# Experts: the last block's rows added from the chip, all other rows fetched under its computation, gates applied at the copy

## The reference, cut to what matters

```
# hier_moe(xf [T, 1024], ...):  T = 768 tokens in layer 0 (512 latent + 256 context), 512 in layer 1
# 4 groups x 8 experts; each token picks one group and its 2 best experts
gate = jax.nn.softmax(top_v, axis=-1) * g_val            # one gate per token and choice
# the 2*T (token, choice) pairs are sorted by expert into blocks of rows
yb  = (silu(xblk @ w1[e]) * (xblk @ w3[e])) @ w2[e]      # per block; w1, w3 [1024, 512], w2 [512, 1024]
out = zeros.at[row_tok].add(yb * row_gate[:, None])
# then   x = x + g2 * out        (g2: a scale per channel)
```

## Time and profile before

| | us |
|---|---|
| median of 3 runs (lowest, highest) | 3034.67 (3034.35, 3039.01) |
| the profiled execution | 3035.01 |
| its span in the profile | 3033.1 |
| PE busy in the span | 2746.8 (91%) |
| DVE, ACT, POOL busy | 1291.5, 842.7, 214.4 |
| layer 0: first to last `silu` of the blocks | 1619.98 to 2100.63 |
| layer 1: the same | 2537.55 to 2994.92 |
| least distance of two `silu`s (a block that nothing holds up) | 13.5 |
| the last two distances in layer 0; in layer 1 | 14.61, 15.28; 14.99, 15.75 |

### The profile page before, as it was taken

How to read it: one execution, slowest core, us unless ns; L and a number is a source line. 1 busy time by engine, 2 the same in 40 slices (tenths; PEclk the granted TensorE clock), 3 DMA queues, 4 the chain that set the end, 5 groups by cost and what they waited for, 6 DMA issues and landing times. The chain is left out here.

```text
span 3033.1 us, 33241 instructions
## 1 busy us (share of the span) xinstructions
PE 2746.8 (91%) x12578; PEld 1791.7 (59%) x12578; DVE 1291.5 (43%) x2005; ACT 842.7 (28%) x1404; POOL 214.4 (7%) x304
## 2 busy tenths in 40 slices
PE   7999989999989999899978988987797987998986
PEld 5888867766767888688654433333664553433332
DVE  5776575655456766621452111111647732111112
ACT  3323235454343323322221111111325721111110
POOL 0111100000001111012100000000000000000000
PEclk9999999999999999999988999998898997999998
DMA  5666622211225566511058999998110047999997
GB/s 205 216 223 223 220 77 70 84 58 68 97 76 208 194 213 234 185 55 69 15 210 348 423 426 424 426 427 352 68 48 15 1 203 315 423 426 425 424 426 270
DMA packets 104597, 672.57 MB, mean 222 GB/s; under 512 B 14712, under 2 KB 19192, under 8 KB 50224
## 3 DMA queue, kind: packets, MB, share of 16 engines
q1 hardware_dynamic: 65360, 542.64, 44.4%
q0 software_dynamic: 32800, 105.12, 9.7%
q10 hardware_dynamic: 6336, 23.50, 2.1%
HBM read 685.91 MB, written 24.64 MB: 234 GB/s over the span
## 5 line engine op out<-in xcount | busy, mean ns | idle before, releaser
L2306 DVE TENSOR_TENSOR big<-big,bank 64x512 f32<-64x512 f32 x65 | 44.9, 691 | 811.5 <-ACT big L1543 811.5
L1973 DVE SCALAR_TENSOR_TENSOR tabs<-tabs,tmp 128x1024 f32<-128x1024 f32 x160 | 193.6, 1223 | 174.8 <-DMA tabs<-in_wm 174.4
L949 PE MATMUL bank<-big 128*64 128x512 f32 x464 | 215.9, 620 | 37.1 <-DMA big<-in_w 35.5
L952 PE MATMUL bank<-big 128*64 128x512 f32 x512 | 237.5, 618 | 0.0
L949 PE MATMUL bank<-slot,big 128*64 128x512 f32 x480 | 211.4, 593 | 2.9 <-DMA ar_f<-in_w 2.9
L952 PE MATMUL bank<-ar_f,big 128*64 128x512 f32 x480 | 211.4, 593 | 0.0
L1396 ACT ACTIVATE w_high<-slot 128x1024 fp32r<-128x1024 f32 (+1 forms) x138 | 140.8, 1041 | 203.9 <-DMA slot<-in_w 102.1
L639 PE MATMUL bank<-u_split,w_low 128*128 128x512 f32 x720 | 178.0, 389 | 0.0
L949 PEld LDWEIGHTS bank<-big 128*64 128x64 f32 x464 | 64.5, 143 | 183.2 <-issue 129.0
L965 PE MATMUL bank<-big 128*64 128x512 f32 x560 | 153.9, 701 | 19.2 <-DVE big L2310 19.2
L2736 POOL DMA_DIRECT2D tabs<-in_wm x160 | 84.7, 529 | 1164.8 <-DVE tabs L1973 723.7
(11 more groups left out here) (415 smaller groups left out, 5534.7 us busy)
## 6 DMA issues: line engine op xcount, KB each, us to landing
big<-in_w SPq DMA_DIRECT2D x93, 2048.0 KB
slot<-in_w SPq DMA_DIRECT2D x164, 1024.0 KB, 4.8
tabs<-in_wm POOLq DMA_DIRECT2D x160, 512.0 KB, 4.6
ar_f<-in_w SPq DMA_DIRECT2D x64, 1024.0 KB
tabs<-in_w SPq DMA_DIRECT2D x32, 1024.0 KB
tmp<-in_w SPq DMA_DIRECT2D x32, 1024.0 KB
slot<-in_wd SPq DMA_DIRECT2D x16, 1408.0 KB, 6.4
ar_u<-in_w SPq DMA_DIRECT2D x18, 1024.0 KB, 18.1
```

Source lines behind the costliest of these rows:

```text
L949: ga = nc.tensor.matmul(bank[0][lo, :], xT[:, 4 * c + k, :], w[c][:, k * EF:(k + 1) * EF], **flags)
L952: mm = nc.tensor.matmul(bank[0][hi, :], xT[:, 4 * c + k, :], w[2 + c][:, k * EF:(k + 1) * EF], **flags)
L1973: nc.vector.scalar_tensor_tensor(mslot[m % 2], mslot[m % 2], 1.0, crow, ALU.mult, ALU.mult, accum_out=modf[:, idx:idx + 1]).then_inc(mod_d ...
L2306: nc.vector.tensor_tensor(hmul[MB:2 * MB, :], hsil[MB:2 * MB, :], bank[0][MB:2 * MB, :], ALU.mult).then_inc(q["h_ready"], 1)
```

## The change

1. **Gates.** POOL builds `gate_block`, as `in_block` but with the gate as value, which DVE until now applied to `yrows`. PE multiplies it with `at_place` into a table of gates for each block and row, ACT copies it to `slot_gates`, and `copy_y` applies it as the scale of its copy.
2. **Last block.** It always uses the third set. The registers are set so that the last loop has one block less and the pairs may be one less. SP issues its six loads with no wait. The last loop's wait number is now `2 * n - 1`, which for the first of its blocks means the block before the block before.
3. **Selection.** DVE builds `last_sel`, 64 x 768, one where a row of the last block belongs to a token. At the end PE computes a tile's sum transposed as a product of the fetched rows with the identity plus a product of `ysb`'s rows with `last_sel`. The last block is not scattered.
4. **Fetch.** SP waits for `y_last`, now the scatter of the last block but one, and issues all fetches while the last block is computed. In layer 0 it issues two loads for the attention among them. The meeting of the engines there is gone.
5. **Zeros.** Rows of `yb` that belong to the last block are not written, so POOL clears both layers' `yb` (2 x 6.3 MB) from a tile of zeros after the layer `even_in`.

```diff
@@ SP, stream_experts
+                def fetch(t):
+                    for x in range(2):
+                        rows_of = d["yb"][l][x * SC + t * P:x * SC + t * P + P, :]
+                        sp.dma_start(yrows[t][x], rows_of).then_inc(got[t], 16)
...
+                sp.wait_ge(q["route_sums"], route_sum(l, "gates"))
                 for c in ORDER[4:]:
                     load(c, e2, 2)
...
-                with sp.Fori(2 * pairs + rotated, last + 1) as b:
-                    block_of(b, b, 1)
-                sp.wait_ge(q["gate_full"], last + 1)
+                with sp.Fori(pairs + rotated // 2, last - pairs - rotated // 2) as n:
+                    block_of(nc.s_assert_within(n + pairs + rotated // 2, 14, NBMAX - 2), 2 * n - 1, 1)
+                e_last = sp.value_load(exp_i[0:1, bass.ds(last, 1)], min_val=0, max_val=NE - 1)
+                for c in ORDER:
+                    load(c, e_last, 2)
+                sp.wait_ge(tload[1], 32 * (rotated // 3 + 1) * (l + 1))
+                sp.wait_ge(q["y_last"], 16 * (l + 1))
+                for t in range(LT):
+                    fetch(t)
+                if l == 0:
+                    for c in range(2):
+                        qkv_load(c)
+                    for t in range(LT, TT):
+                        fetch(t)
@@ PE, moe_layer
+                pe.wait_ge(gates_in, l + 1)
+                for n in range(2 * nt):
+                    mm = nc.tensor.matmul(bank[3][:, 0:TABW], at_place[:, n, :], gate_block[:, n, :], start=(n == 0), stop=(n == 2 * nt - 1))
+                mm.then_inc(q["route_sums"], 1)
...
-                phase.end()
+                block(last, in_third(rotated // 3), None, None)
...
+                    if t == 0:
+                        pe.wait_ge(q["sel_ready"], l + 1)
+                        pe.wait_ge(q["y_ready"], last + 1)
                     for k in range(KT):
-                        tr = nc.tensor.transpose(bank[2 * (t % 2) + k // 4][:, (k % 4) * P:(k % 4 + 1) * P],
-                                                 yrows[t][0][:, k * P:(k + 1) * P], ident)
+                        out_k = bank[2 * (t % 2) + k // 4][:, (k % 4) * P:(k % 4 + 1) * P]
+                        nc.tensor.matmul(out_k, yrows[t][0][:, k * P:(k + 1) * P], ident, start=True, stop=False)
+                        tr = nc.tensor.matmul(out_k, ysb[lo, k * P:(k + 1) * P], last_sel[:, t * P:(t + 1) * P], start=False, stop=True)
@@ ACT, moe_layer
-                    nc.scalar.activation(ysb[rows, 0:EF], bank[4][0:MB, :], ACT.Copy)
-                    nc.scalar.activation(ysb[rows, EF:D], bank[4][MB:2 * MB, :], ACT.Copy).then_inc(q["y_ready"], 1)
+                    for n, half in enumerate((slice(0, MB), slice(MB, 2 * MB))):
+                        i = nc.scalar.activation(ysb[rows, n * EF:(n + 1) * EF], bank[4][half, :], ACT.Identity,
+                                                 scale=slot_gates[half, bass.ds(at, 1)])
+                    i.then_inc(q["y_ready"], 1)
...
+                silu(last)
                 act.wait_ge(q["y_last"], 16 * (l + 1))
-                phase.end()
-                for t in range(nt):
-                    if t > 1:
-                        act.wait_ge(q[f"got{t % 2}"], 32 * ((TT * l + t) // 2))
-                    for x in range(2):
-                        rows_of = d["yb"][l][x * SC + t * P:x * SC + t * P + P, :]
-                        act.dma_start(yrows[t][x], rows_of).then_inc(q[f"got{t % 2}"], 16)
+                copy_y(last, lo)
@@ DVE, moe_layer
-                        dve.wait_ge(q[f"got{t % 2}"], 32 * ((TT * l + t) // 2 + 1))
+                        dve.wait_ge(got[t], 32 * (l + 1))
                         first, second = yrows[t]
-                        nc.vector.tensor_scalar(first, first, scal[:, 7, t:t + 1], None, ALU.mult)
-                        dve.drain()
-                        nc.vector.scalar_tensor_tensor(first, second, scal[:, 8, t:t + 1], first, ALU.mult, ALU.add).then_inc(q["sum_ready"], 1)
+                        nc.vector.tensor_tensor(first, first, second, ALU.add).then_inc(q["sum_ready"], 1)
@@ POOL
+                pool.wait_ge(q["routed"], placed(l, 1))
+                for t in range(nt):
+                    for x in range(2):
+                        i = nc.gpsimd.tensor_scalar(gate_block[:, 2 * t + x, :], const("count")[:, 0:TABW], pos_f[:, 1, x, t:t + 1],
+                                                    scal[:, 7 + x, t:t + 1], ALU.is_equal, ALU.mult)
+                i.then_inc(gates_in, 1)
...
+            nc.gpsimd.memset(zeros, 0.0).then_inc(zeros_in, 1)
+            pool.wait_ge(zeros_in, 1)
+            for l in range(2):
+                pool.dma_start(d["yb"][l].rearrange("(p a) b -> p (a b)", p=P).rearrange("p (n z) -> p n z", z=768),
+                               zeros.unsqueeze(1).to_broadcast([P, 2 * SC * D // P // 768, 768])).then_inc(cleared, 16)
```

More of the change, by code:

```diff
@@ L300, in program @@
         in_block = part(m0 + D + 2 * TT * P, [2 * TT, TABW])
+        gate_block = part(rt, [2 * TT, TABW])
         used, tab_f = (part(rt + 2200 + 6 * TT + TABW * n, [TABW]) for n in range(2))
+        slot_gates = sb("slot_gates", [P, TABW])
+        last_sel = slot[0][0:MB, 2048:2048 + SC]
+        last_tok = small[0:MB, 82:83]
+        last_rel = small[0:MB, 0:2 * TT]
+        zeros = slot[1][:, 2048:2048 + 768]
         tab_u = sb("tab_u", [P, TABW], U32)
@@ L355, in program @@
         mdone = [[sem(f"mdone{c}_{l}") for c in range(2)] for l in range(2)]
+        gates_in, gates_ready = sem("gates_in"), sem("gates_ready")
         stored, last_out = sem("stored"), sem("last_out")
+        got = [sem(f"got{t}") for t in range(TT)]
+        zeros_in, cleared = sem("zeros_in"), sem("cleared")
         block = ctx.enter_context(nc.Block())
@@ L368, in loads @@
                 return sload[l][g], 32 * (b // 3 + 2)
-            return tload[g], 32 * ((rotated // 3) * l + b // 3 + 1)
+            return tload[g], 32 * ((rotated // 3 + 1) * l + b // 3 + 1)
         ROUTED = "onehot", "nblk", "cmp"
-        ROUTE_SUMS = "logits", "counts", "ranks", "starts", "exp_row", "tab_full"
+        ROUTE_SUMS = "logits", "counts", "ranks", "starts", "exp_row", "tab_full", "gates"
         def routed(l, step):
@@ L608, in _ @@
             stream_experts(0)
[L609 to L612, removed]
+            for c in range(2, 6):
+                sp.wait_ge(full[(0, 0, 3, 1, 3, 1)[c]], R_QKV + (0, 0, 1, 2, 2, 3)[c])
+                qkv_load(c)
             stream("wo", 2)
@@ L983, in block @@
                     up(b, held, first)
-                    spread_x(b + 1, part, fetched)
+                    if part is not None:
+                        spread_x(b + 1, part, fetched)
                     spread_h(b)
@@ L993, in moe_layer @@
                     block(2 * i + rotated + 1, in_main(i + 6), lo, i + rotated // 2 + 2)
-                with pe.Fori(pairs + rotated // 2, last + 1 - pairs - rotated // 2) as n:
+                with pe.Fori(pairs + rotated // 2, last - pairs - rotated // 2) as n:
                     block(n + pairs + rotated // 2, in_side(n), lo, n + 2)
-                phase.end()
+                block(last, in_third(rotated // 3), None, None)
                 def token_sums(t):
@@ L1543, in silu, with copy_y @@
                     nc.scalar.activation(hsil[MB:2 * MB, :], bank[0][0:MB, :], ACT.Silu).then_inc(q["sg_ready"], 1)
-                def copy_y(b, rows, written=None):
+                def copy_y(b, rows, written=None, at=None):
+                    at = b if at is None else at
                     act.wait_ge(q["w2_done"], b + 1)
@@ L2313, in moe_layer @@
                 last = dve.value_load(exp_i[0:1, TABW:TABW + 1], min_val=2, max_val=NBMAX - 1)
+                nc.vector.tensor_copy(last_tok, tab_u[0:MB, bass.ds(last, 1)])
+                dve.drain()
+                nc.vector.tensor_scalar(last_rel, const("count")[0:MB, 0:2 * TT], -float(MB), last_tok, ALU.mult, ALU.add)
+                dve.drain()
+                nc.vector.tensor_tensor(last_sel.rearrange("p (n r) -> p n r", n=2 * TT), const("count")[0:MB, 0:MB].unsqueeze(1).to_broadcast([MB, 2 * TT, MB]),
+                                        last_rel.unsqueeze(2).to_broadcast([MB, 2 * TT, MB]), ALU.is_equal).then_inc(q["sel_ready"], 1)
                 copy_x(0)
@@ L2320, in moe_layer @@
                 copy_h(1)
-                with dve.Fori(2, last + 1) as b:
+                with dve.Fori(2, last) as b:
                     mul(b)
@@ L2711, in moe_layer @@
                     gather_next(2 * m + 4)
-                with pool.Fori(pairs + rotated // 2 - 1, last + 1 - pairs - rotated // 2 - 1) as m:
+                with pool.Fori(pairs + rotated // 2 - 1, last - pairs - rotated // 2 - 1) as m:
                     b = m + pairs + rotated // 2 + 1
```

29 lines of the change are left out of this document (19 added, 10 removed).

## The result

| | changed kernel | before |
|---|---|---|
| beside each other: median of 4 executions (lowest, highest) | 3069.2 (3062.6, 3083.0) | 3035.4 (3034.4, 3039.0) |
| ratio, 95% interval | 1.0115 (1.0075 to 1.0156) | |
| later, on another occasion: 6 executions | 3070.4 (3041.4, 3084.7); ratio 1.0104 (1.0056 to 1.0152) | 3033.6 |
| profiled execution; its span | 3062.6; 3060.8 | 3035.01; 3033.1 |

The kernel is slower by about 1%, 34 us, where 3024 was forecast. Two things stand out in the times alone. The time is outside the predicted range, and the changed kernel scatters over 20 us in the first four executions and 43 in the later six, where before scatters over 5 to 6.

The account below looks back on a forecast made before the run. PE was busy 91% of the span, but the layer ends were read as waits on scatter, fetch and DVE. Layer 1 -8.6, layer 0 -2.3, routing +0.5 sum to -10.4 us: forecast 3024 us, range 3012 to 3033.

Parts of the forecast that it names:

- the price of a tile: Ends of both layers: a tile's 16 products, 32 PE instructions, take 3.9 us at full clock, 7.6 at half.
- The rival of half clock: Both layer ends: waits between tiles keep PE's clock at 0.50, +34 us, 3069 us; chance 0.05.
- one behind the other, ran at 0.96: Argument against half clock: at 2136 to 2149, layer 0's end before the change, such products ran at 0.96.
- Layer 1 from the last `out`: End of layer 1: 26.0 us from last `out` to end, against 31.6 before; with the earlier weight stream -8.6 us.
- rival of full cover: Both layers: rows ready before the copy, clock stays, stream gains fully, no routing cost; 3014 us, chance 0.20.
- late row: Both layer ends: last scatter or gather lands late, PE starts 5 us after `out`; 3032 us, chance 0.14.
- the 1.5 for a falling clock: Both layer ends: 1.5 us added (between 0 and 2.6) because PE's wait may let its clock fall.
- Layer 0 from the last `out`: End of layer 0: 40.1 us through six tiles and their sums, against 41.7 before, 1.6 us less.
- The weights: Weight stream in the last blocks: layer 1 gains 3.0 us without its pause; layer 0 keeps its pause, gains 0.7.
- Routing: Before the blocks, both layers: PE's added gate products hidden behind the gather; +0.5 us, ends 0 and 2.8.
- the upper end of 2.8: Routing's worst: 0.3 us more, plus 2.5 if POOL's 3.6 us began only at 1602.2 and PE's 5.4 followed.
- Gates and clearing: Scaled copy the same size as before (0.59 us); clearing 12.6 MB while DMA is idle costs 0, at most 3 us.

Follow-up runs that it names:

- grouped kernel: Changed kernel with each tile's eight products of fetched rows first, then the eight of the last block, not in turns: 3018.5 us, ratio 0.9946 against the kernel before.
- experiments 4 and 5: Changed kernel with turns in one layer only, the other grouped: layer 0 alone 3031.5 to 3056.8 us; layer 1 alone median 3046.0 us.
- experiment 2: Changed kernel, products still in turns, but the last block's also 128 rows deep, with zeros in the selection: 3016.7 us, ratio 0.9939 against the kernel before.
- experiment 9: Kernel before with one part added: gates at ScalarE's copy alone 3031.6 us, ratio 0.9992; clearing of the row buffers alone 3033.0 us, ratio 0.9998.
- experiment 8: Changed kernel with the last block scattered, the fetch waiting for it, and transposes in place of products: 3026.5 us, ratio 0.9976 against the kernel before.
- experiment 7: Changed kernel without the last block's products (its rows missing from the output), fetched rows transposed: 3004.8 us, ratio 0.9902 against the kernel before.

## Why the prediction was wrong, by its steps

**The step that failed** is the price of a tile: "At full clock 16 take 1.95 us, so a tile's 16 products, 32 instructions, take 3.9." The row was read rightly, but it is a train of products that are all 128 rows deep. Half of the new ones are 64 deep and every neighbour differs. The price holds for the grouped order (3.96 measured) and is 6.67 for the order in the code, over the 6 us that the prediction itself gave as its sign of being wrong. For ten tiles that is 27 us. On the grouped kernel's 3018.5, which is what the other terms come to, that makes 3045; by their times, the two executions near 3042 are what the change costs without the next point.

In the first profile the two stretches from the last `out` took 51.5 and 52.7 us where the prediction had 26.0 and 40.1. That is 38.1 us too much, as much as that execution missed by in all (its span is 3060.8 where the sum gave 3033.1 - 10.4 = 3022.7).

**The clock.** The rival of half clock named the right stretch, and its 3069 is the measured median, but by another sum (its tile was 7.6 us and is 11.6, with the changes of depth in it, and in layer 0 it holds in part of the executions). That the numbers agree is luck. It was to come from PE waiting between tiles, and what spoke against it was that PE would be kept busy. PE was, and the clock fell. The argument "one behind the other, ran at 0.96" took PE's being busy in the records as the reason for the high clock; in layer 1 PE was as busy, and the clock was 0.50. The experiments show that the fall comes with the changes of depth: with 16 per tile in layer 1 alone, nine executions of nine by their times, in the changed kernel eight of ten; with 8 per tile two of ten; with 2 or none, none of 13. How the changes do it isn't shown, nor whether other slow trains would do the same.

The profiles add when it falls. In the four stretches that fell (layer 1 of the changed kernel twice, experiments 4 and 5) the clock went down 0.8 to 3.2 us after the first product. In the two that held (layer 0 of the changed kernel, both profiles) the first three tiles, 20 us of turns with no sum between them (2109.28 to 2129.25), ran at 1.00. So the sums, which are 128 deep and come behind the third tile, can't have kept the clock up there at the start. Why it holds there in about half of the executions, and why two executions escaped in layer 1, isn't settled.

**Layer 1 from the last `out`.** PE's start was taken at 3.1 us and is 1.7, as in the rival of full cover; there was no late row. With grouped products the whole stretch is 3022.2 - 2998.8 = 23.4 us, against 26.0 predicted and 31.6 before. So the sum was right without the depth, and a little careful: 1.4 us of the start and the 1.5 for a falling clock weren't needed.

**Layer 0 from the last `out`.** Predicted 40.1 against 41.7 before. With grouped products it is 36.4 us, since PE starts after 1.7 in place of 3.5 and the clock term is nothing again. In the changed kernel it is 52.7, and 52.7 - 36.4 = 16.3 is the price of six tiles (6 x 2.7) with the clock at full.

**The weights.** -3.0 in layer 1: the blocks took 2.0 to 2.4 us less in seven of the ten profiles with the new order, and -0.4 to +0.7 in three. Right in kind, -2.1 in place of -3.0. In layer 0, -0.7 was predicted and +1.8 measured; over those ten profiles it is -1.0 to +2.8, so no gain shows there.

**Routing.** From the start of the long train of table products to `spread_x` it is 1605.87 - 1593.81 = 12.06 us, 11.48 before; in layer 1 9.41 against 9.24. Together +0.75, predicted +0.5: in layer 0 the gather no longer ends last, PE's own gate products do. GpSimd's twelve small operations took 7.54 us together, 0.63 each and not 0.3, and PE waited 1.82 us for them. Beside DVE's small operations each took 0.67 to 0.75 us, behind them 0.56 to 0.64; DVE's own took 0.27 to 0.33 (before 0.28 to 0.31). So GpSimd was slower beside DVE but not held up by it: it began at 1592.98, in the middle of DVE's series, and the upper end of 2.8 didn't come.

**Gates and clearing.** The clearing is the predicted 0. That the prediction took DVE's shorter tile as no gain of its own, since PE takes over, was right.

From the kernel before to the version of experiment 2 the medians go 3033.6 - 2.1 (gates, experiment 9) - 5.0 (to experiment 8) - 21.7 (early fetch, to experiment 7) + 11.9 (products) = 3016.7. Each term is the difference of two neighbours, so the sum closes by itself. The 5.0 holds the order of the weights, the meeting of the engines that is gone and the fetches' move to SP; no run separates them.

## What to carry to other kernels

A price per instruction holds for a train of one shape. Where two kinds of products alternate, look whether their depth (rows of the contraction) is the same; if not, group them, or fill the shallower one with zeros to the full depth: here that costs nothing and saves 0.19 us at 2.4 GHz for each change. And judge a kernel with a clock at stake by several executions, since one may show either level.

## What the runs showed of the hardware

- A change between 128 and 64 rows of depth costs 0.193 us at 2.4 GHz, linear over 2, 8 and 16 changes per tile (3.96, 5.12 and 6.67 us, against 3.57 with none).
- A product of 64 rows takes as long as one of 128: in the grouped order 1.98 us for sixteen instructions of either (3002.47 to 3004.45, 3004.45 to 3006.43).
- The granted clock was 0.50 with PE busy in the records 35.00 of 35 us (3015 to 3050), and 1.00 in the same train of products in layer 0 (38.00 of 38 us, 2110 to 2148). Busy in the records does not mean that the clock stays.
- GpSimd's `tensor_scalar` on 128x57 elements took 0.67 to 0.75 us while DVE ran small operations of its own, and 0.56 to 0.64 behind them (layer 0 of the changed kernel).
